# A three-block transformer kernel: the last sums of squares at both MLP ends and at the last norm, rearranged

## The reference

```
def rmsnorm(x, g):
    y = x32 * lax.rsqrt(jnp.mean(x32 * x32, axis=-1, keepdims=True) + EPS)
    return y * g
h = h + mixer(rmsnorm(h, norm_mix[i]))
h = h + jnp.square(relu(rmsnorm(h, norm_mlp[i]) @ w_in)) @ w_out
...
x = x + g1 * _rmsnorm(_hybrid_mixer(h), norm_g[l, 1])
x = x + g2 * _rmsnorm((gelu(conv(a)) * g) @ w_down, norm_g[l, 3])
```

## Time and profile before

| | us |
|---|---|
| three runs | 2148.09, 2146.18, 2146.72 (median 2146.72) |
| the profiled execution, its time | 2146.94 |
| its span in the trace | 2145.2 |
| TensorE busy | 2064.4 (96% of the span) |
| VectorE busy | 1161.0 (54%) |
| ScalarE busy | 748.6 (35%) |
| GpSimd busy | 583.8 (27%) |

### The profile page before, as it was taken

The page is one execution under the profiler, slowest core; times in us unless marked ns, Lnnn a source line. Parts: engine busy times, 40 slices in busy tenths (PEclk is TensorE's granted clock), DMA queues, the critical chain, the costliest instruction groups (busy, mean ns, idle before and its releaser), DMA issues.

```text
span 2145.2 us, 23937 instructions
## 1 busy us (share of the span) xinstructions
PE 2064.4 (96%) x9444; PEld 1641.4 (77%) x9444; DVE 1161.0 (54%) x1163; ACT 748.6 (35%) x783; POOL 583.8 (27%) x478
## 2 busy tenths in 40 slices
PE   8999999999999998999999998999999979999996
PEld 5666777777777887777777776788888858888884
DVE  4687455655655445455655654594235354545455
ACT  4455432222225432332222223345553233322322
POOL 0000189994000000189994001233320000000000
PEclk9999999999999999999999998999999989999998
DMA  4200144442222231134442222132222312222221
GB/s 173 87 20 1 40 150 145 148 148 95 98 79 81 79 98 40 40 141 153 149 146 96 98 79 84 60 79 64 75 79 98 107 51 99 80 96 98 98 98 39
DMA packets 30812, 197.81 MB, mean 92 GB/s; under 512 B 3312, under 2 KB 3440, under 8 KB 7952
## 3 DMA queue, kind: packets, MB, share of 16 engines
q1 hardware_dynamic: 25552, 168.44, 23.0%
q0 software_dynamic: 5184, 28.31, 4.0%
HBM read 191.50 MB, written 2.10 MB: 90 GB/s over the span
## 4 chain that ended last, share of the span: by engine, by line
PE 85%; DVE 7%; issue 4%; ACT 3%; POOL 1%; DMA 0%; DVEq 0%; POOLq 0%; ACTq 0%; SPq 0%
PE ps L252 23%; PE ps L254 22%; PE ps L253 22%; PE ps L551 3%; PE ps L333 2%; DVE x L808 2%; PE ps L538 1%; PE ps L1391 1%; PE ps L283 1%; PE ps L285 1%; PE ps L284 1%; PE ps L941 1%; PE ps L530 1%; PE ps L529 1%; DVE m_r L816 1%
## 5 line engine op out<-in xcount | busy, mean ns | idle before, releaser
L222 DVE TENSOR_TENSOR w_lo<-w_raw,w_hi 128x2048 fp32r<-128x2048 f32 x140 | 326.4, 2332 | 218.1 <-ACT w_hi L214 216.5
L214 ACT ACTIVATE w_hi<-w_raw 128x2048 fp32r<-128x2048 f32 x144 | 275.3, 1912 | 411.7 <-PE ps L254 411.6
L252 PE MATMUL ps<-h_hi,w_hi 128*128 128x512 f32 x944 | 382.2, 405 | 11.8 <-DVE h_lo L380 7.8
L253 PE MATMUL ps<-h_lo,w_hi 128*128 128x512 f32 x944 | 373.6, 396 | 0.0
L254 PE MATMUL ps<-h_hi,w_lo 128*128 128x512 f32 x944 | 372.9, 395 | 0.0
L343 POOL TENSOR_TENSOR sq<-sq 128x1024 f32<-128x1024 f32 x12 | 38.6, 3218 | 857.6 <-ACT sq L320 857.6
L1184 POOL TENSOR_SCALAR ada_t<-ada_w,prm 128x256 f32<-128x256 f32 x192 | 259.1, 1349 | 10.4 <-DMA ada_w<-in_ada 9.5
L252 PEld LDWEIGHTS ps<-h_hi,w_hi 128*128 128x128 f32 x944 | 181.2, 192 | 56.7 <-issue 20.2
L252 PE MATMUL ps<-m_hi,w_hi 128*128 128x512 f32 x512 | 205.4, 401 | 6.5 <-DVE x L808 6.4
L254 PEld LDWEIGHTS ps<-h_hi,w_lo 128*128 128x128 f32 x944 | 180.7, 191 | 39.2
L253 PEld LDWEIGHTS ps<-h_lo,w_hi 128*128 128x128 f32 x944 | 181.3, 192 | 37.5 <-issue 1.4
(11 more groups left out here) (278 smaller groups left out, 3335.9 us busy)
## 6 DMA issues: line engine op xcount, KB each, us to landing
w_raw<-in_wb SPq DMA_DIRECT2D x154, 1024.0 KB, 4.9
ada_w<-in_ada POOLq DMA_DIRECT2D x24, 1024.0 KB, 5.4
x<-in_xT SPq DMA_DIRECT2D x4, 512.0 KB, 5.1
out_T<-x SPq DMA_DIRECT2D x4, 512.0 KB, 2.8
b_k<-b_k POOLq DMA_DIRECT2D x4, 256.0 KB, 5.5
b_kl<-b_kl POOLq DMA_DIRECT2D x4, 256.0 KB, 6.7
con<-in_con SPq DMA_DIRECT2D x1, 640.0 KB, 11.4
a_kh<-a_kh POOLq DMA_DIRECT2D x2, 256.0 KB, 3.7
```

The lines of the kernel that those rows point to most:

```text
L214: act.activation(w_hi[:, slot], w_raw[:, slot], ACT.Copy).then_inc(hi_done, 1)
L222: dve.tensor_tensor(w_lo[:, slot], w_raw[:, slot], w_hi[:, slot].bitcast(F32), ALU.subtract).then_inc(split_done, 1)
L252: pe.matmul(out, w[0], h[0], start=start, stop=False)
L253: pe.matmul(out, w[0], h[1], start=False, stop=False)
```

## The change

Five edits:

1. For norms 2, 4 and 8 (`APART`), piece 2 of the squares is written to a buffer of its own: `m_r[:, 0]` at the MLPs, `f_r[:, 1]` at the feed-forward (`third_square`). So it no longer waits for GpSimd's first fold. It is made in two halves of 128x512.
2. VectorE adds it to `sq[:, 0]` (`dve_fold`), in its order between the adds of quarter 2 and quarter 3; GpSimd keeps the first fold alone.
3. Piece 3 goes to `sq[:, 1]` once the first fold is done, also in two halves, and each half raises a semaphore (`n_half`, then `n_sq`), so TensorE's third matmul can start on the first half.
4. The load of the table set stands ahead of the squares in `mlp_act`, `ffn_act` and ahead of `act_proj` with `i` = 2.
5. At the MLPs `next_hi` moves from behind piece 3 to ahead of it. At norm 6 the `w_hi` of the feed-forward's second block moves from behind piece 3 to behind `act_std`.

```
--- before.py
+++ after.py
@@ -287,6 +287,8 @@
                     after(t)
             return last.then_inc(block_done, 1) if count else last
 
+        two = lambda ap: ap.rearrange("p (a s) -> p a s", a=2)
+
         def pair_(i):
             return ps[:, 2 * i:2 * i + 2, :]
 
@@ -307,8 +309,25 @@
         def square_slot(n, j):
             return min(j, 1) if n in FOLDED else j % 2
 
+        APART = (2, 4, 8)
+        n_half = sem("n_half")
+
+        def third_square(n):
+
+            return (ff["f_r"][:, 1] if n == 8 else ml["m_r"][:, 0]).rearrange("p (a s) -> p a s", a=2)
+
         def act_square(act, n, j, src):
 
+            if n in APART and j >= 2:
+                if j == 3:
+                    act.wait_ge(n_fold, 2 * FOLDED.index(n) + 1)
+                to = third_square(n) if j == 2 else two(sq[:, 1])
+                for i in range(2):
+                    ins = act.activation(to[:, i, :], src[:, 2 * j + i, :], ACT.Square)
+                    if j == 3 and i == 0:
+                        ins.then_inc(n_half, 1)
+                ins.then_inc(n_sq, 1)
+                return
             if j >= 2 and n in FOLDED:
                 act.wait_ge(n_fold, 2 * FOLDED.index(n) + j - 1)
             elif j >= 2:
@@ -326,21 +345,29 @@
                 return
             if folded and j == 2:
                 pe.wait_ge(n_fold, 2 * FOLDED.index(n) + 2)
-            else:
+            elif not (n in APART and j == 3):
                 pe.wait_ge(n_sq, 4 * n + j + 1)
             slot = j - 2 if folded else j % 2
             for i in range(2):
+                if n in APART and j == 3:
+                    pe.wait_ge(*((n_half, APART.index(n) + 1) if i == 0 else (n_sq, 4 * n + 4)))
                 last = pe.matmul(ps[:, bank, :], ones[:], squares(n)[:, slot, i * S:(i + 1) * S],
                                  start=(j == (2 if folded else 0) and i == 0), stop=(j == 3 and i == 1))
             last.then_inc(n_ssq, 1)
 
         def pool_fold(pool, n):
 
-            for j in (1, 2):
+            for j in (1,) if n in APART else (1, 2):
                 pool.wait_ge(n_sq, 4 * n + j + 1)
                 if j == 2:
                     pool.wait_ge(n_fold, 2 * FOLDED.index(n) + 1)
                 pool.tensor_tensor(sq[:, 0], sq[:, 0], sq[:, 1], ALU.add).then_inc(n_fold, 1)
+
+        def dve_fold(dve, n):
+
+            dve.wait_ge(n_sq, 4 * n + 3)
+            dve.wait_ge(n_fold, 2 * FOLDED.index(n) + 1)
+            dve.tensor_tensor(two(sq[:, 0]), two(sq[:, 0]), third_square(n), ALU.add).then_inc(n_fold, 1)
 
         def act_std(act, n, bank):
 
@@ -443,7 +470,7 @@
                 if i < 2:
                     mlp_hi(act, i, j)
                 act_square(act, n, j, src)
-                if j == 3:
+                if j == 3 and i < 2:
                     next_hi(act, b + 2, b % 2)
 
         def dve_proj(dve, i, b0, dst, add):
@@ -466,7 +493,6 @@
         a_S, a_top, a_exp, a_T, a_pt, a_PV, a_ln, a_inv_s, a_on, a_oh, a_ol = map(sem, (
             "a_scores", "a_max", "a_exp", "a_turned", "a_p_turned", "a_pv", "a_ln", "a_inv_s", "a_o_norm", "a_o_hi", "a_o_lo"))
         V_BLOCK = N_QKV - 1
-        two = lambda ap: ap.rearrange("p (a s) -> p a s", a=2)
         NU = 4 * 16
         a_q2 = at_["a_q2"][:].rearrange("p (t r) s -> p t r s", r=2)
         a_out = (a_q2[:, :, 0, :], a_q2[:, :, 1, :])
@@ -791,10 +817,12 @@
                 turn(it)
             u = MLP_UNITS - 1
             mlp_act_in(act, i, u, u % 2, b0 + 2 * u - 1, (b0 + 1) % 2)
+            act.preload_act_table_set("natural_log_exp_and_others")
             for q in range(4):
+                if q == 3:
+                    next_hi(act, b0 + 2 * u + 3, (b0 + 1) % 2)
                 act.wait_ge(m_add, 4 * (MLP_UNITS * i + u) + q + 1)
                 act_square(act, n, q, x)
-            next_hi(act, b0 + 2 * u + 3, (b0 + 1) % 2)
 
         def mlp_dve_add(dve, i, u, q, b):
             c = MLP_UNITS * i + u
@@ -842,6 +870,8 @@
             u = MLP_UNITS - 1
             mlp_dve_in(dve, i, u, u % 2, b0 + 2 * u - 1, (b0 + 1) % 2)
             for q in range(4):
+                if q == 3:
+                    dve_fold(dve, 2 * i + 2)
                 mlp_dve_add(dve, i, u, q, b0 + 2 * u + 1)
             next_lo(dve, b0 + 2 * u + 3, (b0 + 1) % 2)
 
@@ -2040,6 +2071,8 @@
             u = FFN_UNITS - 1
             unit(u, b0 + 3 * u - 1, u, last=True)
             for q in range(4):
+                if q == 3:
+                    dve_fold(dve, 8)
                 add(u, q, b0 + 3 * u + 2)
 
         def renorm_squares(act, n, src):
@@ -2140,21 +2173,20 @@
         e["act_proj"](act, 0, B_WO0, 1, x, 6)
         e["act_std"](act, 1, 6)
         e["mlp_act"](act, 0, B_MLP0, 2)
-        act.preload_act_table_set("natural_log_exp_and_others")
         e["act_norm_h"](act, 2, 1, 2)
         e["gla_act"](act, B_GLA)
         e["act_proj"](act, 1, B_WO1, 3, x, 6)
         e["act_std"](act, 3, 6)
         e["mlp_act"](act, 1, B_MLP1, 4)
-        act.preload_act_table_set("natural_log_exp_and_others")
         e["act_std"](act, 4, 2)
         e["renorm_squares"](act, 5, x)
         e["act_norm_h"](act, 5, 2, 2, shift(0))
         e["mix_act"](act, B_MIX)
         e["merge_act"](act, B_MERGE)
+        act.preload_act_table_set("natural_log_exp_and_others")
         e["act_proj"](act, 2, B_WOUT, 6, e["y"], 6)
-        act.preload_act_table_set("natural_log_exp_and_others")
         e["act_std"](act, 6, 6)
+        e["split_hi"](act, B_FFN + 1, (B_FFN + 1) % 2)
         e["renorm_squares"](act, 7, x)
         e["act_norm_h"](act, 7, 3, 2, shift(1))
         e["ffn_act"](act, B_FFN, 8)
```

5 lines of the change are left out of this document (2 added, 3 removed).

## The result

| | before | changed |
|---|---|---|
| runs beside each other | 6 | 6 |
| median us | 2146.45 | 2134.77 |
| lowest and highest us | 2145.83, 2151.43 | 2131.25, 2137.90 |
| profiled execution us (span) | 2146.94 (2145.2) | 2136.50 (2134.7) |

The ratio is 0.994, with a 95% interval of 0.9924 to 0.9956: faster by 0.6%, or 11.7 us. In the later group of e1 the changed kernel had 2136.63 (6 runs) against 2146.61 (17 runs), ratio 0.9951 (0.9937 to 0.9966), 10.0 us. As gains the two intervals are 9.4 to 16.3 us and 7.3 to 13.5.

The account below looks back on a forecast made before the run. TensorE, busy for 96% of the span, was taken as the bound, idle at the norms. Terms 1.47 + 1.47 + 1.05 + 1.67 + 1.30 = 7.0, plus 0.5 for the clock, made 7.5 us: 2139.2 us, range 2136.5 to 2142.3.

Parts of the forecast that it names:

- MLP 1, MLP 2, each: At each MLP end, sums start 1.56 us earlier through VectorE's fold, less 0.09 waiting for the fourth square: 1.47 us.
- norm 6: At norm 6, Ln starts when the sums end, no longer behind ScalarE's weight copy and table load: 1.05 us.
- norm 8, sums: At norm 8, the program's tail, sums start 1.76 us earlier, less 0.09 for the fourth square's first half: 1.67 us.
- norm 8, table: At norm 8, the table load of 1.28 us between Ln and Exp goes, with its step: 1.30 us.
- rival (d): The switch of tables is dearer than its row by another 1.28 us: 2137.9 us; chance 0.03.
- the clock's term in the paragraph on MLP 2: At MLP 2's sums, a third of the 1.53 us lost to the clock's fall is regained: 0.5 us, ends 0 and 1.53.
- Rival (b): Clock falls inside the earlier narrow matmuls or lasts longer, at one or two ends, 1.6 us each: 2141.3 to 2142.9; chance 0.10.
- Rival (a): Clock gives more: whole 1.53 us at MLP 2, 2138.2; with one low stretch shorter behind an end, 2136.6; chance 0.12.
- (c): MLP ends pass nothing on, the next block being held by something fixed; only norms 6 and 8 count: 2142.7; chance 0.06.
- (e): At the MLP ends the fourth square sticks behind a weight copy waiting for its DMA: slower, up to 2154.3; chance 0.03.

Follow-up runs that it names:

- e1: The changed kernel again, unaltered, with a second profile: 2136.63 us, the kernel before 2146.61.
- e2: The kernel before with only the table loads moved and norm 6's weight copy behind Exp: 2142.96 us, ratio 0.9982.
- e5: The kernel before with spare wide matmuls where TensorE was idle at the norms, and one per four narrow matmuls: 2139.86 us.
- e10: The kernel before with spare matmuls behind norm 0's and 5's sums and ahead of and behind norm 7's: 2142.02 us.
- e11: The kernel before with norm 6's edit alone (table load ahead of the projection, weight copy behind Exp): 2143.05 us, ratio 0.9983.
- e4: The changed kernel with the third and fourth square in one piece each in place of halves: 2132.90 us.
- e13: The kernel before with 9 spare wide matmuls in the idle time ahead of the sums of norms 2, 4 and 8: 2143.86 us, ratio 0.9981.
- e8: The changed kernel with the first 8 of the 48 narrow matmuls moved ahead of the sums: 2129.47 us.
- e12: The changed kernel with the weight copy behind the fourth square again at both MLP ends: 2133.13 us.
- e3: The changed kernel with the table loads and norm 6's weight copy put back, VectorE's fold kept: 2139.33 us.
- e7: The changed kernel with spare matmuls only where TensorE is idle, behind norm 0's, 5's, 7's sums and ahead of 7's: 2126.82 us, ratio 0.9904.
- e9: The changed kernel with spare matmuls only where TensorE is idle and 8 narrow matmuls ahead of the sums: 2126.56 us.
- e14: The kernel of e7 (changed kernel with spares only in idle time) again, beside e15 on one chip: 2130.02 us.
- e15: The kernel of e9 (idle spares and 8 narrow matmuls ahead) again, beside e14 on one chip: 2125.51 us, ratio 0.9897.
- e6: The changed kernel with spare wide matmuls at the gaps, fewer where idle stretches are shorter, and among the narrow matmuls: 2133.28 us.

## Why the prediction was wrong

**The steps of the path: right, each a little small.**

| term | forecast | read from the two profiles |
|---|---|---|
| MLP 1, MLP 2, each | 1.47 | 2.67 - 0.96 of idle time, less 0.08 in the sums: 1.63 |
| norm 6 | 1.05 | 1.04 |
| norm 8, sums | 1.67 | 2.86 - 0.96, less 0.07: 1.83 |
| norm 8, table | 1.30 | 1.28 |
| sum | 7.0 | 7.4 |

The surplus at the three ends, 0.16 each, is nearly all one number: two halves of a square take 1.15 us, and I had taken 1.29 from two copies to another type. VectorE's add took 1.22 to 1.23, the choice among the bounds that was made. The third matmul waited 0.08, the forecast being 0.09. For the table load, the Trainium skill's figure (ScalarE: Activation LUTs, What ACT_TABLE_LOAD costs) would have been 2.66, the load and a drain. The trace shows no drain: it has 1.28 before, and 1.28 gone after, so rival (d) falls.

**The step that failed is the clock's term in the paragraph on MLP 2.** I took 0.5 us, a third of the one fall seen, and let the range hold 1.53 and one stretch more. Two things were wrong.

First, the sums. The kernel before can lose the clock at each of its three ends, and these runs don't say when. Five profiles have such an end as it was, behind 2.66 to 2.87 us of idle time. TensorE's sums there, in us:

| profile | MLP 1 | MLP 2 | norm 8 |
|---|---|---|---|
| before | 3.70 | 5.23 | 3.70 |
| e2 | 5.40 | 5.26 | 3.70 |
| e5 | filled | filled | 5.15 |
| e10 | 6.76 | 3.70 | 5.11 |
| e11 | 3.70 | 6.78 | 3.70 |

The mean excess over 3.70 is 1.06 per end, 3.2 us for three. With 13 readings it is an estimate, uncertain by some 2 us either way. Behind 0.96 us or less the sums of the changed kernel and of the versions made from it took 3.77 or 3.78 in every one of 24 readings (without e4, whose sums have the gap shown above, and without the MLP ends with narrow matmuls ahead, where they took 3.68). Behind filled idle time the kernel before took 3.70 in all five (e5, e13). I had three readings and counted them with equal weight, but gave the term to one end only, although nothing in the rows set that end apart from the other two; and none of the three had yet shown 6.8. That alone is worth some 3.2 in place of 0.5, and e13, which takes away only this, measured 3.4 (1.9 to 6.2).

Second, norm 7, which I didn't price at all. Norm 6's edit moved Ln by 1.05 and so cut TensorE's wait ahead of norm 7's sums from 6.88 to 5.84. In all seven profiles with 5.84 or 5.85 (the changed kernel twice, e2, e4, e8, e11, e12) these sums took 8.90 or 8.91, and in the three with 6.88 (before, e3, e13) 10.08, 9.96 and 9.94. Behind them the low stretch is one of 3.4 us in the former and 6.8 in the latter. By the shifts between the traces, that is 1.0 to 1.2 in the sums and 1.05 behind them: 2.2 us. e11 measured 3.7 for a step of 1.05. Why a wait shorter by 1.05 does this is not shown.

**The new account:** 7.4 + 3.2 + 2.2 = 12.8. Measured: 11.7 and 10.0, with both intervals around 12.8. In the profiled pair something is taken back at MLP 1, where the narrow matmuls took 7.48 against 5.91, 1.6 us. Rival (b) named this place and this price. But that, too, is one draw: over both MLP ends, the narrow matmuls took 5.91, 5.79, 7.82, 5.77, 7.49, 8.03, 5.73 and 7.47 in before, e2, e10 and e11, 6.75 in the mean, against 7.00 in the mean of the eight readings in the changed kernel's two profiles, e3 and e12. With single readings from 5.7 to 8.0 on both sides it is not shown that the change costs anything there. Rival (a) had the gain of the clock at up to 3.1 us; by this account it is 5.4. I held (a) and (b) against each other as cases, when both happened in one execution.

A smaller slip lies in the prices of these rivals. I read the low stretches behind MLP 2 as 3.2 and 6.4 us long. A granted clock of 0.58 over 1 us, between levels of 0.5 and 1, means 0.84 us at the low one; by that the same rows give 3.4 and 6.8, the first from 1291.16, the second from 1301.4. At half speed the shorter is worth 1.7 and not 1.6.

**The others.** Rivals (c) and (e) fall: TensorE has no idle time between the sums and the next block, and the copy started at 644.59, when TensorE's last quarter was done, with no wait for its weights. The weight copy ended only 0.03 us ahead of the add that the fourth square also waits for, and not 0.27: the halves of the third square ended sooner, so the fold and the add did, but the copy didn't.

**Still open:** why e10 is 15 us behind e7 and e9. Steps of 7.4, sums of 3.2 and, for e9, 1.9 for the narrow matmuls make 10.6 to 12.5; 3 to 5 us are not accounted for by these means. The profiles of e10 and e7, 14.8 us apart, show the places. In that pair the sums differ by 4.5, so steps and sums make 11.9. From norm 2's Ln to the next Ln, in the linear attention, e10 takes 1.4 more (182.77 and 181.33), and from norm 4's Ln to norm 5's 1.1 more (16.73 and 15.60), both with longer stretches of low clock. Whether the change or chance makes these stretches shorter was not tested. When within idle or narrow work the clock falls was not settled either; the same idle time gave either outcome.

## What to carry to other kernels

Where TensorE is idle or nearly so for some microseconds in the midst of dense work, price the clock behind the gap as its own term, at every such place, by readings from several executions; one profile shows one draw. In this kernel shortening three gaps from some 2.7 to 1.0 us gave 5.3 us of waiting and, by an estimate from 13 readings, 3.2 us more in the clock of the sums behind them. And then fill what stays idle: spare matmuls in gaps that can't be closed gave 5 to 10 us on top of the change by the medians of different groups (e7, e14), though on the kernel before only 4.7 (e10).

## What the runs showed of the hardware

At both MLP ends of every profile a stretch of low clock begins among the 48 matmuls of one column or within 0.7 us of their end, 3.4 to 10.2 us long. TensorE has no gap there but one of 0.5 us at MLP 2 where 8 of them were moved ahead (e8, e9, e15). Where the 48 stand together they took from 5.42 to 8.17 us, the longer the more of them ran at 1.2 GHz. One wide matmul (0.23 us) per four narrow ones didn't prevent it (e5, e6). The spread of the kernel before over all its runs, 2140.99 to 2151.65, goes with the mean granted clock: the fastest of these runs had 0.984, the slowest 0.978. With spares at the gaps and among the narrow matmuls the kernel before spreads over 2.8 us (e5) and the changed one over 0.9 (e6); with spares in the gaps alone the changed one still spreads over 4.9 and 6.2 (e7, e14).
